# Six half slots for the sparse experts' raw weights, and the dense experts' weights spread between the gathers

## The chip, the cores and the metric

One core of one Trainium2 chip. The metric is the device time of one execution in microseconds (us), as the median of several runs. The engines are TensorE (PE, with its weight loads as PEld), VectorE (DVE), ScalarE (ACT), GpSimd (POOL) and SyncE (SP), which here only issues the weight loads. L584 is line 584 of the kernel before.

## The reference, cut to what matters

Two transformer blocks run one after the other over 256 tokens of 1024 features, in float32. The change touches only the last step of the second block, a mixture of 16 experts in 4 groups:

```python
gsel = jnp.argmax(glog, axis=-1)                       # one group a token
top_p, top_i = lax.top_k(ep, TOPK_IN_GROUP)            # two of its four experts
comb = jnp.sum(jax.nn.one_hot(eid, N_EXPERTS) * wts[..., None], axis=1)
act = jax.nn.silu(jnp.einsum("nd,edf->nef", xt, w1)) * jnp.einsum("nd,edf->nef", xt, w3)
act = act * comb[:, :, None].astype(act.dtype)
y = jnp.einsum("nef,efd->nd", act, w2)                 # D_EXPERT = 256, d = 1024
```

## The kernel before, in words

**Weights.** All weight matrices lie in one stream in HBM, cut into quarters of 128 x 1024 float32. SP loads them two at a time, as halves of 1 MB, into `raw`, a ring of six quarters, so three halves. A quarter is then split in two float32r parts, so that three fast matmul passes give nearly the float32 result: ScalarE rounds it to `w_hi` and another engine subtracts to get `w_lo` (both rings of six quarters as well, with the same index `ring(n)`). In most of the kernel that other engine is GpSimd (L538); in the stage of the sparse experts it is VectorE (`slot_low`, L2381). TensorE's `three` (L962 to 968) issues the three passes; nearly all matmuls have L967. `quarter_done` counts the quarters that TensorE has finished.

**The two dense experts.** Experts 0 and 1 of group 0 are computed for all 256 tokens (`expert_up`, then four row quarters, "the dense down"). Their activations `e_act` are multiplied by each token's weight. For that `comb` is transposed (L1556), stored as `comb_t` (L2361), spread over the partitions with `selectors` (L1561) and multiplied in (L2366); ScalarE rounds to `g_hi` (L918) and VectorE makes `g_lo` (L2372).

**Gathers.** Tokens are sorted by group into 5 tiles of 128 slots: one for each group, and a spare one for a group with more than 128 tokens. One-hot matrices gather the tokens' rows (`tok_hi`, `tok_lo`) into `slot_hi` and `slot_lo`. For each of the 8 feature blocks k a gather of 4 matmuls of 512 columns writes one of banks 4 to 7; ScalarE rounds it (L910), VectorE takes the rest (L2352). After that 8 small gathers of 128 columns do the spare tile (L914, L2357). L1566 gathers the experts' weights for each slot; L2368 sums them to `slot_weight`.

**The sparse experts.** 18 expert slots follow, (tile, expert), each with four up quarters (q0 to q3: gate and up together) and two down quarters. Of these q4 is split like the others; q5, called WHOLE, is used in plain float32 straight from `raw` (L1629, four passes long), so its slot in `raw` is free only when TensorE is done with it. `SLOT_ORDER` puts the down quarters of an expert behind the up quarters of the next: up(0); then up(s), down(s-1) for s = 1 to 17; then down(17). ScalarE and VectorE split four quarters ahead of TensorE (`LEAD`). Between q1 and q2 of up(s) TensorE turns the activations of s-1 (`turn_act`, L1602 to 1607), ScalarE copies them out (L925, L926) and VectorE makes their `g_lo` (L2396). SILU and product are L941 and L2390. At the end matmuls scatter the results back to the tokens (L1639), and a last norm and the store follow.

**Order of the loads.** SP issues in order. Half h of the sparse stage goes to slot (N_HALVES + h) % 3 of `raw` and waits until the half three before it has been used up:

```python
sp.wait_ge(sem("slot_lo_done"), split_count(2 * h - 4))
if SLOT_ORDER[2 * h - 5][1] == WHOLE:
    sp.wait_ge(sem("quarter_done"), N_QUARTERS + 2 * h - 4)
```

Each engine runs its own list in the order in which it is written, so a wait holds back all that stands behind it on that engine.

Of the kernel before, what the change touches and what calls it, by code (L numbers as in the profile page):

```python
# [84 lines left out]
SLOT_HALVES = len(SLOT_ORDER) // 2  # L85

# [5 lines left out]
def split_count(i):  # L92

    return sum(q != WHOLE for _, q in SLOT_ORDER[:i])
# [211 lines left out]
def program(nc, weights, smalls, x_in, p_in, vec_in, rows, con_in, slot_in, sel_in, pos_in, out):  # L306

    ctx = ExitStack()
    with ctx:
# [14 lines left out]
        w_lo = sb("w_lo", RING * QUARTER, F32R)  # L324
        h_hi = sb("h_hi", KD * S, F32R)
# [103 lines left out]
        slot_silu, slot_act = e_act[:, 0:S], e_act[:, S:2 * S]  # L429
        tok_hi = [x[:, 4:8, :].rearrange("p k s -> p (k s)") for x in (g_hi, g_lo)]  # L430
# [58 lines left out]
        def _(sp):  # L489
# [19 lines left out]
            for h in range(SLOT_HALVES):  # L509
                s, q = SLOT_ORDER[2 * h]  # L510
                tile, expert = EXPERT_TILES[s]
                if h < 3:
                    sp.wait_ge(sem("lo_done"), N_QUARTERS + 2 * h - 4)
                else:
                    sp.wait_ge(sem("slot_lo_done"), split_count(2 * h - 4))
                    if SLOT_ORDER[2 * h - 5][1] == WHOLE:
                        sp.wait_ge(sem("quarter_done"), N_QUARTERS + 2 * h - 4)
                at = N_HALVES + 3 * expert + q // 2
                if tile < GROUPS:
                    load_half(at + 3 * GROUP_EXPERTS * tile, (N_HALVES + h) % 3)  # L520
                else:
                    if (expert, q) == (0, 0):
                        sp.wait_ge(sem("overflow_ready"), 1)
                        spare = sp.value_load(overflow_group[0:1, :], min_val=0, max_val=GROUPS - 1)
                    load_half(spare * (3 * GROUP_EXPERTS) + at, (N_HALVES + h) % 3)
# [23 lines left out]
        def _(act_e):  # L549
# [27 lines left out]
            def slot_hi_quarter(i):  # L577
# [4 lines left out]
                act_e.wait_ge(sem(f"half_loaded{n % RING // 2}"), (n // RING + 1) * 16)  # L582
                act_e.wait_ge(sem("quarter_done"), n - (RING - 1))
                nc.scalar.activation(w_hi[:, ring(n)], raw[:, ring(n)], ACT.Copy).then_inc(sem("slot_hi_done"), 1)  # L584
# [323 lines left out]
            for k in range(KD):  # L908
                act_e.wait_ge(sem("gathered"), k + 1)
                nc.scalar.activation(slot_hi[:, k, 0:GROUPS, :], bank[4 + k % 4][:, :].rearrange("p (t c) -> p t c", c=P), ACT.Copy,  # L910
                                     scale=v("norm2", k)).then_inc(sem("slot_h_hi"), 1)
# [4 lines left out]
            for i in range(DENSE):  # L916
                act_e.wait_ge(sem("expert_act_ready"), i + 1)
                nc.scalar.copy(g_hi[:, 2 * i:2 * i + 2, :], e_act[:, i, :]).then_inc(sem("expert_hi_done"), 1)  # L918
# [40 lines left out]
        def _(pe):  # L959
# [579 lines left out]
            expert_up(1)  # L1539
            pe.wait_ge(sem("one_hot_ready"), NT)  # L1540
            pe.wait_ge(sem("tok_lo_done"), NT)
            for k in range(KD):
                if k >= 4:
                    pe.wait_ge(sem("slot_h_lo"), k // 2 * 2 - 2)
                gather(bank[4 + k % 4][:, :], k, slice(0, GROUPS * P)).then_inc(sem("gathered"), 1)
# [7 lines left out]
            pe.wait_ge(sem("pair_free1"), 42)  # L1553
            pe.wait_ge(sem("comb_ready"), NT)
            for t in range(NT):
                ins = nc.tensor.transpose(bank[3][0:N_EXPERTS, t * P:(t + 1) * P], comb[:, t, :], ident)  # L1556
            ins.then_inc(sem("comb_turned"), 1)
            pe.wait_ge(sem("comb_t_stored"), 1)
            pe.wait_ge(sem("selectors_loaded"), 16)
            for e in range(DENSE):  # L1560
                ins = mm(bank[2][:, e * S:(e + 1) * S], selectors[0:N_EXPERTS, e * P:(e + 1) * P], comb_t, start=True, stop=True)  # L1561
            ins.then_inc(sem("comb_spread"), 1)
            pe.wait_ge(sem("comb_slots_ready"), 1)
            for j in range(TILES):
                for t in range(NT):
                    ins = mm(bank[3][:, S + 16 * j:S + 16 * (j + 1)], one_hot[:, t, j * P:(j + 1) * P].bitcast(F32),  # L1566
                             comb_slots[:, t, :], start=t == 0, stop=t == 1)
            ins.then_inc(sem("comb_gathered"), 1)
# [40 lines left out]
            def slot_down(i, s, q):  # L1609
# [14 lines left out]
                else:  # L1624
                    pe.wait_ge(sem(f"half_loaded{n % RING // 2}"), (n // RING + 1) * 16)
                    pe.wait_ge(sem("slot_act_copied"), 2 * s + 2)
                    whole = raw[:, ring(n)]
# [37 lines left out]
        def _(dve):  # L1665
# [684 lines left out]
            for k in range(KD):  # L2350
                dve.wait_ge(sem("slot_h_hi"), k + 1)
                V.scalar_tensor_tensor(slot_lo[:, k, 0:GROUPS, :], bank[4 + k % 4][:, :].rearrange("p (t c) -> p t c", c=P),  # L2352
                                       v("norm2", k), slot_hi[:, k, 0:GROUPS, :].bitcast(F32), ALU.mult, ALU.subtract)\
                    .then_inc(sem("slot_h_lo"), 1)
# [5 lines left out]
            dve.wait_ge(sem("comb_turned"), 1)  # L2360
            V.tensor_copy(comb_t, bank[3][0:N_EXPERTS, 0:S]).then_inc(sem("comb_t_stored"), 1)  # L2361
            dve.wait_ge(sem("comb_spread"), 1)
            for i in range(DENSE):
# [108 lines left out]
```

## Time and profile before

| | us |
|---|---|
| median of 3 runs | 1007.19 |
| lowest, highest | 1005.96, 1010.86 |
| profiled execution | 1007.87 |
| its span in the trace | 1006.1 |
| TensorE busy | 884.3 (88%) |
| VectorE, ScalarE, GpSimd busy | 466.6, 436.5, 470.1 |
| weights moved | 155.20 MB on SP's queue |

A row of a timeline or a group gives the instruction's start and length, what it writes and reads, and in brackets how long its engine sat idle before it and what ended that. The ends of matmuls are modelled: in a stream a 512-column matmul shows 0.39 us, while the next one starts 0.23 us after it. A chain of waits goes back from the last instruction, at each step to what released it. The granted clock is 1.00 at 2.4 GHz and 0.50 at 1.2 GHz. The gathers, the spreading and the dense down stand at 743.6 to 777.2 us, the sparse experts at 777.2 to 990.4 us.

### The profile page before, as it was taken

Reading aid. Unit: us, or ns where it says so; the run is one execution under the profiler, and the core shown is the slowest. Engines: PE = TensorE matmul, PEld = TensorE weight load, DVE = VectorE, ACT = ScalarE, POOL = GpSimd, SP = SyncE. Lnnn points to the kernel's source line nnn. Section 1 sums busy time; section 2 is a strip of 40 time slices with the busy share of each in tenths; the row PEclk is TensorE's granted clock in tenths of the full one; section 3 lists DMA queues with packets and bytes.
Section 4 is the critical chain, followed back from the end, with each engine's and each line's share of the span. In section 5 each row is a group of like instructions: output and inputs, shape, how many; then the busy total and the mean of one; then the engine's idle time right before and its main releaser. Section 6 shows DMA issues by size and latency. Waiting matters only on the chain.

```text
span 1006.1 us, 16140 instructions
## 1 busy us (share of the span) xinstructions
PE 884.3 (88%) x6246; PEld 766.9 (76%) x6246; DVE 466.6 (46%) x962; ACT 436.5 (43%) x676; POOL 470.1 (47%) x372
## 2 busy tenths in 40 slices
PE   4999977999999975999997989989798988888884
PEld 4888867999999864998787989877697765555553
DVE  3723354121112156339456344562784755555643
ACT  5264324454455443534661332333453545445531
POOL 5786664888998954665452233458440000000000
PEclk9999988999999997999988999989897999999998
DMA  7542523555555533243321122235232576766651
GB/s 288 211 146 107 168 100 130 178 200 171 204 168 190 184 126 126 89 164 127 126 85 43 49 80 85 86 126 205 86 127 83 219 305 272 279 262 252 251 209 42
DMA packets 23548, 159.59 MB, mean 159 GB/s; under 512 B 2992, under 2 KB 3520, under 8 KB 4800
## 3 DMA queue, kind: packets, MB, share of 16 engines
q1 hardware_dynamic: 21584, 155.20, 42.3%
q10 hardware_dynamic: 1904, 3.54, 1.0%
q8 instruction: 44, 0.72, 0.3%
q14 instruction: 16, 0.13, 0.0%
HBM read 157.68 MB, written 1.05 MB: 158 GB/s over the span
## 4 chain that ended last, share of the span: by engine, by line
PE 67%; DVE 17%; DMA 9%; ACT 3%; issue 2%; ACTq 0%; SPq 0%; DVEq 0%
PE bank L967 48%; DMA raw<-weights_dram 8%; PE bank L1629 4%; PE bank L1369 3%; DVE w_lo L2381 2%; ACT w_hi L584 2%; PE bank L1056 1%; PE bank L1044 1%; PE bank L1534 1%; DMA row<-dt_bias_dram 1%; DVE work L1755 1%; PE bank L1639 1%; DVE tok L1695 1%; DVE stat L1681 1%; DVE stat L1680 1%
## 5 line engine op out<-in xcount | busy, mean ns | idle before, releaser
L538 POOL TENSOR_TENSOR w_lo<-raw,w_hi 128x512 fp32r<-128x512 f32 x368 | 469.9, 1311 | 274.6 <-ACT w_hi L575 274.3
L967 PE MATMUL bank<-h_hi,w_hi 128*128 128x256 f32 x856 | 250.1, 292 | 0.8 <-POOL w_lo L538 0.8
L967 PE MATMUL bank<-h_lo,w_hi 128*128 128x256 f32 x856 | 243.6, 285 | 0.0
L967 PE MATMUL bank<-h_hi,w_lo 128*128 128x256 f32 x856 | 243.3, 284 | 0.0
L575 ACT ACTIVATE w_hi<-raw 128x1024 fp32r<-128x1024 f32 x184 | 188.6, 1056 | 95.5 <-PE bank L967 80.4
L967 PEld LDWEIGHTS bank<-h_hi,w_hi 128*128 128x128 f32 x856 | 165.4, 193 | 6.3 <-issue 2.5
L967 PEld LDWEIGHTS bank<-h_lo,w_hi 128*128 128x128 f32 x856 | 165.6, 193 | 0.8 <-issue 0.5
L967 PEld LDWEIGHTS bank<-h_hi,w_lo 128*128 128x128 f32 x856 | 165.4, 193 | 0.0
L2381 DVE TENSOR_TENSOR w_lo<-raw,w_hi 128x1024 fp32r<-128x1024 f32 x90 | 106.9, 1221 | 85.3 <-ACT w_hi L584 85.3
L584 ACT ACTIVATE w_hi<-raw 128x1024 fp32r<-128x1024 f32 x90 | 91.7, 1053 | 104.0 <-DMA raw<-weights_dram 92.3
L967 PE MATMUL bank<-w_hi,g_hi 128*128 128x512 f32 x172 | 70.6, 410 | 29.9 <-DVE g_lo L2396 29.0
L1879 DVE SCALAR_TENSOR_TENSOR work<-bank,vec,work 128x255 f32<-128x255 f32 (+1 forms) x44 | 19.2, 478 | 111.1 <-ACT work L664 109.8
L967 PE MATMUL bank<-w_hi,g_lo 128*128 128x512 f32 x172 | 69.6, 405 | 0.0
L967 PE MATMUL bank<-w_lo,g_hi 128*128 128x512 f32 x172 | 69.1, 402 | 0.0
L967 PEld LDWEIGHTS bank<-w_hi,g_hi 128*128 128x128 f32 x172 | 33.3, 194 | 42.8 <-DVE w_lo L2381 28.5
L967 PE MATMUL bank<-w_hi,slot_hi 128*128 128x512 f32 x144 | 65.3, 454 | 0.0
L967 PE MATMUL bank<-w_hi,h_hi 128*128 128x512 f32 (+1 forms) x144 | 56.9, 395 | 4.2 <-issue 2.2
L967 PE MATMUL bank<-w_hi,slot_lo 128*128 128x512 f32 x144 | 56.9, 395 | 0.0
L967 PE MATMUL bank<-w_lo,slot_hi 128*128 128x512 f32 x144 | 56.8, 395 | 0.0
L1044 PE MATMUL bank<-con,tok 128*128 128x128 f32 x80 | 19.0, 418 | 42.7 <-DVE tok L1695 30.7
L967 PE MATMUL bank<-w_lo,h_hi 128*128 128x512 f32 (+1 forms) x144 | 55.1, 383 | 0.0
L967 PE MATMUL bank<-w_hi,h_lo 128*128 128x512 f32 (+1 forms) x144 | 55.1, 383 | 0.0
(347 smaller groups left out, 1311.0 us busy)
## 6 DMA issues: line engine op xcount, KB each, us to landing
raw<-weights_dram SPq DMA_DIRECT2D x146, 1024.0 KB, 4.9
x_sb<-x_dram SPq DMA_DIRECT2D x2, 512.0 KB, 4.7
work<-final_norm_dram ACTq DMA_DIRECT2D x2, 512.0 KB, 4.9
out_dram<-tok SPq DMA_DIRECT2D x1, 1024.0 KB, 4.0
work<-constants_dram ACTq DMA_DIRECT2D x1, 640.0 KB, 6.6
con<-constants_dram ACTq DMA_DIRECT2D x1, 584.0 KB, 5.3
work<-slot_constants_dram ACTq DMA_DIRECT2D x1, 454.0 KB, 5.6
work<-p_dram ACTq DMA_DIRECT2D x1, 256.0 KB, 6.7
```

Of the source, the lines that this page charges most:

```text
L538: ins = nc.gpsimd.tensor_tensor(w_lo[:, part], raw[:, part], w_hi[:, part].bitcast(F32), ALU.subtract)
L575: nc.scalar.activation(w_hi[:, ring(q)], raw[:, ring(q)], ACT.Copy).then_inc(sem("hi_done"), 1)
L584: nc.scalar.activation(w_hi[:, ring(n)], raw[:, ring(n)], ACT.Copy).then_inc(sem("slot_hi_done"), 1)
L967: ins = mm(dst, a, b, start=start and n == 0, stop=stop and n == 2, skip_group_check=True)
L1044: ins = nc.tensor.transpose(bank[4 + k // 2][:, k % 2 * S + t * P:k % 2 * S + (t + 1) * P], tok3[:, t, k * P:(k + 1) * P], ident)
L1056: ins = mm(bank[4 + n % 2][:, t * P:t * P + (t + 1) * P], q3[at:at + HD, f, t * P:(t + 1) * P], k3[at:at + HD, kf(f), 0:(t + 1) * P], star ...
L1369: ins = mm(bank[b][rows, column + m * w:column + (m + 1) * w], lhs[rows, m, :], rhs[rows, m, :], start=True, stop=True)
L1534: ins = mm(dst, x[t][:, k * P:(k + 1) * P], one_hot[:, t, of], start=t == 0 and x is tok_hi, stop=t == 1 and x is tok_lo, skip_group_check ...
L1629: ins = mm(y_banks(tile)[c][:, :], g_whole, whole[:, c * 512:(c + 1) * 512], start=False, stop=last_of_tile(s), skip_group_check=True)
L1639: ins = mm(total[t, c][:, :], one_hot_t[:, tile, t * P:(t + 1) * P], y[:, tile, c * 512:(c + 1) * 512], start=tile == 0 and y is y_hi, sto ...
L1879: ins = V.scalar_tensor_tensor(c, u, fvec("conv_w", (f + j) * 3 + 2 - back), c, ALU.mult, ALU.add)
L2381: V.tensor_tensor(w_lo[:, ring(n)], raw[:, ring(n)], w_hi[:, ring(n)].bitcast(F32), ALU.subtract)\
```

## The change

Two things are changed, both in the mixture of experts. Every computation stays, with its shapes.

First, the raw halves of the sparse stage go round six slots instead of three: the three of `raw`, two in the space of `h_hi` and `h_lo` (here `spare`), free after the dense experts' up projections, and one in `tok`, free after the last gather. Half h waits for what was freed by half h-6, and each slot has its own semaphore. `w_hi` and `w_lo` keep their rings of six quarters.

Second, the transposes of `comb`, the spread, and the gather of the slots' weights move from behind all gathers to between them: the transposes ahead of the first gather, the spread after four, the slots' weights after eight, then the small gathers. VectorE and ScalarE get their parts in a matching order.

```diff
+SLOT_RING = 6
+        def slot_raw(h):
+            r = h % SLOT_RING
+            if r < RING // 2:
+                half = (N_HALVES + r) % (RING // 2)
+                return raw[:, 2 * half * QUARTER:2 * (half + 1) * QUARTER]
+            if r < RING // 2 + 2:
+                return spare[:, (r - RING // 2) * 2 * QUARTER:(r - RING // 2 + 1) * 2 * QUARTER]
+            return tok[:, :]
@@ SP
-                if h < 3:
+                if h < RING // 2:
                     sp.wait_ge(sem("lo_done"), N_QUARTERS + 2 * h - 4)
+                elif h < RING // 2 + 2:
+                    sp.wait_ge(sem("quarter_done"), 4 * (B_MOE + 2))
+                elif h < SLOT_RING:
+                    sp.wait_ge(sem("gathered"), KD + 2)
                 else:
-                    sp.wait_ge(sem("slot_lo_done"), split_count(2 * h - 4))
-                    if SLOT_ORDER[2 * h - 5][1] == WHOLE:
-                        sp.wait_ge(sem("quarter_done"), N_QUARTERS + 2 * h - 4)
+                    freed = 2 * (h - SLOT_RING) + 2
+                    sp.wait_ge(sem("slot_lo_done"), split_count(freed))
+                    if SLOT_ORDER[freed - 1][1] == WHOLE:
+                        sp.wait_ge(sem("quarter_done"), N_QUARTERS + freed)
...
+                sp.dma_start(slot_raw(h), src).then_inc(sem(f"slot_loaded{h % SLOT_RING}"), 16)
@@ ScalarE, slot_hi_quarter
-                act_e.wait_ge(sem(f"half_loaded{n % RING // 2}"), (n // RING + 1) * 16)
+                act_e.wait_ge(sem(f"slot_loaded{i // 2 % SLOT_RING}"), (i // 2 // SLOT_RING + 1) * 16)
                 act_e.wait_ge(sem("quarter_done"), n - (RING - 1))
@@ ScalarE, gathers (rounding of k = 0 to 7; before: all eight, the spare tile, then g_hi)
+            slot_h_first(range(6))
+            for i in range(DENSE):
+                act_e.wait_ge(sem("expert_act_ready"), i + 1)
+                nc.scalar.copy(g_hi[:, 2 * i:2 * i + 2, :], e_act[:, i, :]).then_inc(sem("expert_hi_done"), 1)
+            slot_h_first(range(6, KD))
@@ TensorE (before: all of this behind the small gathers)
+            pe.wait_ge(sem("pair_free1"), 42)
+            pe.wait_ge(sem("comb_ready"), NT)
+            for t in range(NT):
+                ins = nc.tensor.transpose(bank[3][0:N_EXPERTS, t * P:(t + 1) * P], comb[:, t, :], ident)
...
+            gather_groups(range(4))
+            pe.wait_ge(sem("comb_t_stored"), 1)
+            pe.wait_ge(sem("selectors_loaded"), 16)
+            for e in range(DENSE):
+                ins = mm(bank[2][:, e * S:(e + 1) * S], selectors[0:N_EXPERTS, e * P:(e + 1) * P], comb_t, start=True, stop=True)
+            ins.then_inc(sem("comb_spread"), 1)
+            gather_groups(range(4, KD))
+            pe.wait_ge(sem("comb_slots_ready"), 1)
...
+            ins.then_inc(sem("comb_gathered"), 1)
@@ VectorE (before: all slot_lo, then these)
+            dve.wait_ge(sem("comb_turned"), 1)
+            V.tensor_copy(comb_t, bank[3][0:N_EXPERTS, 0:S]).then_inc(sem("comb_t_stored"), 1)
+            slot_h_second(range(4))
+            dve.wait_ge(sem("comb_spread"), 1)
+            (the two products with e_act)
+            slot_h_second(range(4, KD))
+            (g_lo, slot_weight, then the spare tile)
```

## Rows read from the trace of the kernel before

**Rows 1.** The page: granted TensorE clock in 40 equal slices, tenths.

```profile
PEclk9999988999999997999988999989897999999998
```

**Rows 2.** Chain of waits, one expert: start us, us, what.

```profile
813.66 4.79 DMA raw<-weights_dram
818.48 1.07 ACT w_hi L584
819.57 1.22 DVE w_lo L2381
820.80 0.21 DVE g_lo L2396
...
821.15 1.62 PE bank L967 x6
822.77 1.73 PE bank L1629 x4
```

**Rows 3.** Waits, 777 to 990 us: total us, times, longest.

```profile
ACT w_hi L584 <- DMA raw<-weights_dram: 92.3, 49, 5.9
...
PE bank L967 <- DVE g_lo L2396: 29.0, 16, 2.1
```

**Rows 4.** By stretch: us; busy PE, PEld, DVE, ACT, POOL; clock; DMA; GB/s.

```profile
230.00:240.00 10.00, 10.00 (x81) 9.81 (x80) 1.47 (x4) 3.88 (x5) 8.52 (x8) 1.00 0.63 204
743.61:754.57 10.96, 10.96 (x67) 9.46 (x66) 7.73 (x13) 6.65 (x12) 1.33 (x2) 1.00 0.32 114
758.00:764.00 6.00, 5.77 (x24) 4.92 (x22) 1.48 (x4) 3.12 (x4) 0.00 (x0) 0.50 0.00 0
764.75:777.20 12.45, 12.45 (x48) 10.18 (x49) 5.22 (x5) 3.18 (x3) 0.00 (x0) 0.88 0.38 124
782.79:791.85 9.06, 9.06 (x38) 6.75 (x37) 7.01 (x9) 5.92 (x9) 0.00 (x0) 1.00 0.63 233
777.20:990.40 213.20, 184.18 (x691) 129.36 (x689) 118.84 (x134) 102.49 (x153) 0.00 (x0) 0.94 0.63 244
```

**Rows 5.** DMA, 780 to 980 us: 40 slices of 5 us; median landing.

```profile
GB/s 98 321 134 419 138 428 157 387 229 321 311 61 429 165 383 223 184 433 125 433 85 315 315 233 392 36 400 205 334 297 105 424 131 411 190 200 428 100 321 3
...
raw<-weights_dram SPq DMA_DIRECT2D x49, 1024.0 KB, 6.9
```

**Rows 6.** Chain of waits, last scatters and last whole down quarter.

```profile
979.70 5.51 PE bank L1639 x24
...
988.64 1.73 PE bank L1629 x4
```

**Rows 7.** TensorE's timeline after the gathers: start, us, ..., [idle before].

```profile
754.57 0.38 PE L1556 MATMUL bank<-con,work 128*16 128x128 f32 x2
757.43 1.96 PE L1561 MATMUL bank<-work 16*128 16x256 f32 x4 [2.49 <-DVE work L2361]
759.32 4.45 PE L1566 MATMUL bank<-work,one_hot 128*128 128x16 f32 x20
764.75 0.77 PE L967 MATMUL bank<-w_hi,g_hi 128*128 128x512 f32 x1 [0.98 <-issue]
```

**Rows 8.** VectorE's timeline in the gather stage.

```profile
743.64 1.27 DVE L2348 TENSOR_TENSOR work<-work,bank 128x512 f32<-128x512 f32 x2
745.47 0.75 DVE L2352 SCALAR_TENSOR_TENSOR slot_lo<-bank,vec,slot_hi 128x512 fp32r<-128x512 f32 x1 [0.56 <-ACT slot_hi L910]
...
755.94 1.12 DVE L2357 SCALAR_TENSOR_TENSOR slot_lo<-bank,vec,slot_hi 128x128 fp32r<-128x128 f32 x4 [0.66 <-ACT slot_hi L914]
...
763.97 1.28 DVE L2372 TENSOR_TENSOR g_lo<-work,g_hi 128x512 fp32r<-128x512 f32 x2
```

**Rows 9.** ScalarE's timeline in the gather stage.

```profile
744.75 0.69 ACT L910 ACTIVATE slot_hi<-bank,vec 128x512 fp32r<-128x512 f32 x1 [3.18 <-PE bank L1534]
...
754.76 1.14 ACT L914 ACTIVATE slot_hi<-bank,vec 128x128 fp32r<-128x128 f32 x4 [0.65 <-PE bank L1534]
760.15 1.22 ACT L918 CAST g_hi<-work 128x512 fp32r<-128x512 f32 x2 [4.25 <-DVE work L2366]
```

More of the change, by code:

```diff
@@ L1551, in _ @@
                     ins.then_inc(sem("gathered"), 1)
[L1553 to L1568, printed above, removed]
             pe.wait_ge(sem("slot_h_lo"), 2 * KD)
@@ L2349, in _, with slot_h_second @@
                     .then_inc(sem(f"pair_free{1 - i}"), 1)
[L2350 to L2354, printed above, removed]
+            dve.wait_ge(sem("comb_turned"), 1)
+            V.tensor_copy(comb_t, bank[3][0:N_EXPERTS, 0:S]).then_inc(sem("comb_t_stored"), 1)
+            def slot_h_second(ks):
+                for k in ks:
+                    dve.wait_ge(sem("slot_h_hi"), k + 1)
+                    V.scalar_tensor_tensor(slot_lo[:, k, 0:GROUPS, :], bank[4 + k % 4][:, :].rearrange("p (t c) -> p t c", c=P),
+                                           v("norm2", k), slot_hi[:, k, 0:GROUPS, :].bitcast(F32), ALU.mult, ALU.subtract)\
+                        .then_inc(sem("slot_h_lo"), 1)
+            slot_h_second(range(4))
+            dve.wait_ge(sem("comb_spread"), 1)
+            for i in range(DENSE):
+                dve.wait_ge(sem(f"pair_free{1 - i}"), 42 + 2 * i)
+                x = e_act[:, i, :].rearrange("p (f s) -> p f s", s=S)
+                V.tensor_tensor(x, x, each_of(bank[2][:, i * S:(i + 1) * S], 2), ALU.mult).then_inc(sem("expert_act_ready"), 1)
+            slot_h_second(range(4, KD))
+            for i in range(DENSE):
+                dve.wait_ge(sem("expert_hi_done"), i + 1)
+                V.tensor_tensor(g_lo[:, 2 * i:2 * i + 2, :], e_act[:, i, :].rearrange("p (f s) -> p f s", s=S),
+                                g_hi[:, 2 * i:2 * i + 2, :].bitcast(F32), ALU.subtract).then_inc(sem("expert_lo_done"), 1)
+            dve.wait_ge(sem("comb_gathered"), 1)
+            V.tensor_reduce(slot_weight, bank[3][:, S:S + 16 * TILES].rearrange("p (t g e) -> p t e g", t=TILES, g=GROUPS),
+                            AX_X, ALU.add).then_inc(sem("slot_weights_ready"), 1)
             for k in range(KD):
@@ L2359, in _ @@
                     .then_inc(sem("slot_h_lo"), 1)
[L2360 to L2363, printed above, removed]
-                dve.wait_ge(sem(f"pair_free{1 - i}"), 42 + 2 * i)
-                x = e_act[:, i, :].rearrange("p (f s) -> p f s", s=S)
-                V.tensor_tensor(x, x, each_of(bank[2][:, i * S:(i + 1) * S], 2), ALU.mult).then_inc(sem("expert_act_ready"), 1)
-            dve.wait_ge(sem("comb_gathered"), 1)
-            V.tensor_reduce(slot_weight, bank[3][:, S:S + 16 * TILES].rearrange("p (t g e) -> p t e g", t=TILES, g=GROUPS),
-                            AX_X, ALU.add).then_inc(sem("slot_weights_ready"), 1)
-            for i in range(DENSE):
-                dve.wait_ge(sem("expert_hi_done"), i + 1)
-                V.tensor_tensor(g_lo[:, 2 * i:2 * i + 2, :], e_act[:, i, :].rearrange("p (f s) -> p f s", s=S),
-                                g_hi[:, 2 * i:2 * i + 2, :].bitcast(F32), ALU.subtract).then_inc(sem("expert_lo_done"), 1)
             def slot_low(i):
```

45 lines of the change are left out of this document (27 added, 18 removed).

## The prediction

> **What bounds the kernel now.** I read the page's clock line first [rows 1], then the chain of waits, then who waited for whom, then busy time by stretch. The page's slices 31 to 39 (755 to 980 us) are the stage of the sparse experts (18 expert slots of three weight halves, 1 MB each). There the granted clock often reads 8 or 9 tenths, where it reads 9 (full) for most of the middle of the kernel.
>
> The chain through one expert [rows 2] is a loop: the whole-float32 quarter of a down projection ends at 813.60, only then does the next half start to load (4.79 us), then ScalarE rounds it (1.07), VectorE takes the rest (1.22), a small g_lo product follows (0.21), TensorE does the down quarter (1.62) and the whole quarter (1.73) to 824.50. That is 10.9 us a turn, and 4.8 of it is a load with nothing in front of it: the half that is wanted next has no free slot until the last one has been used up. The waits say the same [rows 3]: ScalarE waits 92.3 us for loads in 49 waits, and TensorE's idle of 29.0 us is put down to g_lo, the last link of that loop, in 16 waits of up to 2.1 us.
>
> The stretches give the price [rows 4]. From 777.20 to 990.40 TensorE is busy 184.2 of 213.2 us at a mean clock of 0.94. So 29 us are idle, and 0.06 x 213 = 13 us are what running part of the stage at 1.2 instead of 2.4 GHz costs. One turn without idle and at full clock is in the trace: 782.79 to 791.85, 9.06 us, TensorE busy 9.06, VectorE 7.01, ScalarE 5.92. Where TensorE is fed without gaps the clock reads 1.00 (230 to 240 us, and both stretches of full busy time in the gathers and that turn). The Trainium skill says (TensorE: Matmul & The Clock Gate, "What's actually happening") that the lower clock is the array's default and activity releases it; by that rule the 13 us come back with the idle, and the trace agrees in these stretches.
>
> **Part 1, six half slots.** Nothing is removed or added on TensorE, ScalarE or VectorE; 54 loads of the same size stay. What moves is when a load may be issued: half h waits for what freed half h-6, not h-3. Six halves are two experts. In the order of the stage the TensorE's turn is up(s) q0 to q3, down(s-1), whole(s-1). A down half of s-1 waits now for whole(s-3). Call that time T. Behind it in SP's queue stand the two up halves of s+1, whose slots were freed a little before T, so three halves are asked for at about T. Median time to landing with halves in the queue is 6.9 us, and slices of 5 us in this stage moved 428 to 433 GB/s [rows 5], so the three (3.15 MB) need 7.35 us plus the start. Alone, one lands after 4.8 us [rows 2]. The down half is read by ScalarE and VectorE (2.3 us) before TensorE reaches it, at T + 9.06 + 5.8 = T + 14.9. It lands at about T + 5, so 7 to 8 us of cover are left. The up halves of s+1 are wanted at T + 18.1 and land by about T + 10; 6 us of cover. So the load leaves the chain. What is late next? Per turn DMA needs 7.35 us, VectorE 7.01, ScalarE 5.92, TensorE 9.06. TensorE is. The ring of six split quarters is unchanged and runs four quarters ahead; in-order ScalarE does its silu after q3, with the next quarter to be split needed 5.9 us of TensorE work later against about 3.2 us of work (silu 0.4, rounding 1.07, product 0.5, low part 1.22; the first and third are estimates for 256 columns, between ScalarE's 0.28 for 128 and 0.69 for 512 in the rows of part 2), so that should hide too.
>
> The stage then takes: up of the first slot 782.79 - 777.20 = 5.6; 17 turns x 9.06 = 154.0; the end, scatters to the last whole quarter, 979.70 to 990.37 [rows 6], 10.7; five turns that also turn a one-hot tile, two transposes more (0.38 for two at most, [rows 7]; in a stream half of that, the ends being modelled), about 0.2 each, 1.1. Sum 171.4 against 213.2: **41.8 us gained**. Bounds: with the clock not coming back, 13 less; with an added hand-over of 0.3 us a turn, 5 less; it can't be more than about 1 us better, since 9.06 has no idle in it.
>
> A rule that speaks against this: the Trainium skill (SBUF — State Buffer, "Summary: rules for kernel authors") says to reckon with some 358 GB/s for HBM to SBUF. By it three halves take 8.79 us, 0.27 under TensorE's turn, and the sum is the same but with almost no cover. The measured 428 GB/s over whole 5 us slices of this very stage speaks for the higher rate.
>
> The loads issued early cost nothing. Halves 3 and 4 go to the space of h, free when the second dense up ends (743.6); half 5 goes to tok and waits for the last gather, and half 6 on are queued behind it on SP. They wait for nothing lost: half 6 needs the low part of the second slot quarter, which is made beside the dense down. The DMA engines were idle there (0.00 share at 758 to 764, [rows 4]).
>
> **Part 2, the spreading between the gathers.** Before: the gathers run 743.61 to 754.57, then two transposes, 2.49 idle for VectorE's copy of comb_t (queued behind all its slot_lo work), the spread 1.96, the slot weights 4.45 to 763.77, 0.98 idle, and the dense down at 764.75 [rows 7]. The last four items ran at half clock: 0.50 at 758 to 764 [rows 4].
>
> After: TensorE waits first for pair_free1 at 42, the first of the two dense products, which ends 743.64 + 0.64 = 744.3 [rows 8], where before it began at 743.6; everything is queued behind it, price 0.7. The transposes add 0.4: 744.7. Then the same gathers, 10.96, the spread and the slot weights in between. These now stand inside busy time, so at full clock half of 1.96 and of 4.45: 0.98 and 2.2 (bounds: these, or the full 6.4). Sum 744.7 + 10.96 + 3.2 = 758.8. The new waits between gathers: comb_t is copied while four gathers run (3.7). Gather k=6 needs slot_lo of k=3, at about 748.4 + 0.7 + 0.75 + handing over = 750.1 [rows 8, 9], and TensorE comes there at about 751.2. On ScalarE the two g_hi roundings (1.22) stand before k=6 and 7, on VectorE the two products (1.28) before slot_lo of k=4; both have ended before the last gather (VectorE 11.4 us of work, ScalarE 9, in 16.6), so no wait of TensorE comes of them, by estimate. After the last gather the tail stays: 754.57 to the last slot_lo at 755.94 + 1.12 = 757.06, 2.5 us. Then the dense down can begin at 761.3 instead of 764.75, as g_lo and its two roundings have long been done: **3.4 us gained**; bounds 0.2 (everything in between at half clock) and 4.1 (the first wait free).
>
> The dense down took 12.45 at mean clock 0.88 [rows 4], because it began at half clock. Idle of 2.5 us stands just before it in the new order too, as before the drop in the old one, so I leave it at 12.45. Bounds 10.95 (12.45 x 0.88) and 14.
>
> **The sum.** The profiled execution took 1007.87, its span 1006.1. 1007.87 - 41.8 - 3.4 = 962.7. The median of the runs shown is 1007.19, 0.7 less, so **962** for the median after.
>
> **Rivals.**
> A, forecast (TensorE bounds every turn): 962, own range 957 to 968 by the bounds of part 2, the dense down and a few tenths of hand-over in a turn. Chance 0.77.
> B, the loads bound: each turn waits for 3.15 MB at a sustained rate below 3.15/9.06 = 347 GB/s. For it: no long stretch of the stage moved more, and slices such as 315, 315 in a row occur. Against: those fall where nothing was asked for, and full slices reach 428 [rows 5]. At 315 a turn is 9.99, 17 x 0.93 = 16 more: 978. It would show as ScalarE still waiting for slot loads. Chance 0.10.
> C, the clock doesn't come back: the stage has no idle yet keeps stretches at 1.2 GHz: 13 more, 975. Against it 1.00 at 230 to 240 with TensorE full. Chance 0.05.
> D, it doesn't do what it says: SP issues in order, the down half's wait holds back the up halves behind it, and the loads land as late as before. Only part 2 is left: 1003.8. Against: 7 us of cover worked out above. Chance 0.04, with a half-way 985 in it.
> E, slower: with three loads always in the queue, into three separate areas, the sustained rate falls so far that a turn is longer than now. The point: the stage may take 213.2 + 3.4 = 216.6, less the 17.4 outside the turns, over 17 turns, 11.7 us, that is 269 GB/s. At 250 GB/s a turn is 12.6, 17 x 0.9 = 15 us over that point: 1022. For it: landing rises from 4.8 to 6.9 us as loads overlap; against: that is sharing, and the rate rises with it [rows 5]. Chance 0.03. The last 0.01 is for nothing changed.
>
> **How the numbers follow.** A measurement of this kernel can tell about 0.5%, 5 us, from no change. A, B, C, most of D are faster by more: 0.96. D's full case lies 3.4 us below: same 0.02. E: slower 0.02. Range: A with C, and the milder half of B, low 957, high 976; left out are the rest of B, D and E, some 0.12, and what A's range may miss.
>
> **What would show it.** In the trace after: ScalarE's wait for slot loads falls from 92 us to under 10; TensorE has no 2 us waits for g_lo; a turn of 9.1 to 9.3 us; granted clock 1.00 from about 775 on; DMA at a steady 310 to 350 GB/s rather than 430 and 100 in turns. The dense down begins at about 761. The end from the last whole quarter (990.37 before) to the end of the span stays 15.7 us. Wrong if turns stay above 9.6, if SP's queue still asks for each half just before ScalarE wants it, or if waits of 1 us and more stand between the gathers.

## The result, and the profile after

| us | before | after |
|---|---|---|
| median of 4 runs each, side by side | 1007.77 | 972.96 |
| lowest, highest | 1005.96, 1010.86 | 971.08, 974.85 |
| profiled execution | 1007.87 | 974.85 |

The ratio is 0.965, interval 0.961 to 0.969. The forecast was 962, range 957 to 976. A later comparison of the same two programs gave 963.69 (962.14 to 971.99, 5 runs) against 1008.49 and a ratio of 0.954 (0.948 to 0.961). The experiments show where the two medians differ.

Part 1 is to be seen in the chain of waits of after, one expert (start us, us, what), that answers to [rows 2]:

```profile
848.92 2.80 PE bank L995 x12
851.72 0.11 PE bank L1635
851.83 0.11 PE bank L1640
851.93 4.16 PE bank L995 x18
856.10 1.72 PE bank L1662 x4
```

From 848.92 to 857.81, where the next one starts, it is 8.89 us, and every piece is TensorE's: two up quarters, the turning of the activation, two up quarters and the down quarter (18 matmuls), the whole quarter. Load, rounding and g_lo have left the chain. The first five turns, which also turn a one-hot tile, take 9.10 to 9.14 and the eleven behind them 8.88 to 8.91.

The waits of after from 740 to 960 us (us in total, times, longest), to be held beside [rows 3]:

```profile
ACT g_hi L953 <- PE bank L1640: 49.6, 18, 8.4
...
ACT w_hi L607 <- PE bank L995: 10.5, 6, 4.9
...
PE bank L995 <- DVE slot_lo L2410: 2.4, 1, 2.4
...
PE bank L1578 <- DVE work L2381: 1.3, 1, 1.3
```

ScalarE's 92.3 us of waiting for loads are gone. What it waits for now is TensorE: the turned activation (49.6 us) and a free quarter of the ring (10.5). TensorE's 16 waits for g_lo are gone too. Ahead of the last whole quarter it waits twice, both times in the gather stage: 1.3 us before the transposes and 2.4 us before the dense down.

By stretch (columns as in [rows 4]): gathers and spreading, dense down to the last whole quarter, the first 5 us of the dense down, and the turn above.

```profile
753.97:775.23 21.26, 17.64 (x90) 15.35 (x91) 12.87 (x26) 9.83 (x20) 1.77 (x2) 0.80 0.48 182
775.23:957.35 182.12, 182.10 (x738) 136.28 (x738) 124.75 (x138) 105.41 (x156) 0.00 (x0) 0.99 0.72 281
775.00:780.00 5.00, 4.77 (x11) 3.81 (x12) 2.44 (x3) 0.91 (x1) 0.00 (x0) 0.50 0.69 254
848.92:857.81 8.89, 8.89 (x37) 6.57 (x37) 7.99 (x10) 7.42 (x11) 0.00 (x0) 1.00 0.87 341
```

The second row is the main result. TensorE is busy for 182.10 of 182.12 us. The same two events stood 225.6 us apart before (764.75 to 990.37, [rows 6, 7]): 43.5 us less. The first row is the disappointment: from the start of the gather stage to the dense down it is 21.26 us, where it was 21.15 (743.6 to 764.75). The third shows the dense down begin at half clock.

The chain through that stage, which answers to [rows 7]:

```profile
754.47 0.69 DVE work L2381
...
755.20 0.39 PE bank L1578 x2
755.59 3.72 PE bank L1562 x16
759.31 1.05 PE bank L1586 x4
760.36 3.92 PE bank L1562 x16
764.28 2.14 PE bank L1592 x20
766.42 6.43 PE bank L1562 x32
...
773.14 0.89 ACT slot_hi L945 x3
...
774.05 1.14 DVE slot_lo L2410 x4
```

The spread (L1586) takes 1.05 and the slots' weights (L1592) 2.14, both at full clock as forecast. But the 32 small gathers behind them take 6.43 us; before, they were the last part of 10.97 us of gathers, about 3.5 (an estimate: 32 starts 0.11 us apart, the step that the rows below show ahead of 766.9). TensorE's timeline shows the place and the step of the clock. There is no idle of TensorE ahead of it since the transposes began at 755.20:

```profile
764.12 2.30 PE L1592 MATMUL bank<-work,one_hot 128*128 128x16 f32 x20
...
766.75 0.32 PE L1562 MATMUL bank<-one_hot,g_hi 128*128 128x128 f32 x1
766.87 0.42 PE L1562 MATMUL bank<-one_hot,tok_lo 128*128 128x128 f32 x1
767.09 0.41 PE L1562 MATMUL bank<-one_hot,g_lo 128*128 128x128 f32 x1
```

From 766.9 on a 128-column matmul of the gathers starts every 0.21 us instead of every 0.11.

The clock line of the page, and the DMA line from 760 to 960 us (40 slices of 5 us) with the median times to landing, answer to [rows 1, 5]:

```profile
PEclk9999988999999999799998898988989799999998
```

```profile
GB/s 408 7 29 254 136 210 16 378 51 398 274 431 285 419 277 388 326 331 364 306 360 364 433 288 403 329 328 387 310 426 287 419 288 377 364 62 3 0 0 0
...
raw<-weights_dram SPq DMA_DIRECT2D x24, 1024.0 KB, 7.0
spare<-weights_dram SPq DMA_DIRECT2D x16, 1024.0 KB, 5.3
tok<-weights_dram SPq DMA_DIRECT2D x9, 1024.0 KB, 6.9
```

The clock line can't show what the sparse experts gained: in slices 32 to 39 (780 to 981 us) it read 9 before as well, since a 9 is anything from 90% up, and the mean there was 0.94. In after it has a 7 in slice 32 (754 to 778 us, the fall above) and 9 in the seven slices behind it; the window rows say 0.99. It also has more 8s ahead of that, eight instead of six, in code that the change doesn't touch. The tail is as it was (957.35 to the span's end at 973.1, 15.7 us).

So the profiled times differ like this. The gather stage begins 10.4 us later (753.97 against 743.6), its length differs by 0.1, and from the dense down on 43.5 us are gained: 33.0 in all, 1007.87 to 974.85.

### The profile page after: what moved, and what is told of

Same layout as the page of the kernel before. It is cut to its first block, busy times and chain, and to the rows that moved or that the text cites. A ratio compares the mean times of both kernels' runs of the same rounds, so it can differ in the third digit from the quotient of the medians.

```text
span 973.1 us, 16139 instructions
## 1 busy us (share of the span) xinstructions
PE 880.5 (90%) x6246; PEld 773.4 (79%) x6246; DVE 471.8 (48%) x962; ACT 435.8 (45%) x676; POOL 467.0 (48%) x372
## 3 DMA queue, kind: packets, MB, share of 16 engines
HBM read 157.68 MB, written 1.05 MB: 163 GB/s over the span
## 4 chain that ended last, share of the span: by engine, by line
PE 79%; DVE 13%; issue 4%; POOL 3%; ACT 1%; DVEq 0%; POOLq 0%; ACTq 0%
PE bank L995 59%; PE bank L1662 3%; POOL w_lo L561 3%; PE bank L1397 3%; PE bank L1562 1%; PE bank L1072 1%; PE bank L1084 1%; PE bank L1672 1%; DVE stat L1714 1%; DVE stat L1713 1%; DVE work L1948 1%; PE bank L1095 1%; DVE stat L1715 1%; DVE bank L2087 1%; PE bank L1103 1%
## 5 line engine op out<-in xcount | busy, mean ns | idle before, releaser
L598 ACT ACTIVATE w_hi<-raw 128x1024 fp32r<-128x1024 f32 x184 | 188.7, 1056 | 98.1 <-PE bank L995 83.3
L995 PEld LDWEIGHTS bank<-h_hi,w_hi 128*128 128x128 f32 x856 | 167.8, 196 | 7.4 <-issue 3.1
L995 PEld LDWEIGHTS bank<-h_lo,w_hi 128*128 128x128 f32 x856 | 168.2, 196 | 0.8 <-issue 0.5
L995 PEld LDWEIGHTS bank<-h_hi,w_lo 128*128 128x128 f32 x856 | 167.9, 196 | 0.0
L1912 DVE SCALAR_TENSOR_TENSOR work<-bank,vec,work 128x255 f32<-128x255 f32 (+1 forms) x44 | 19.2, 478 | 111.3 <-ACT work L687 109.9
L2420 DVE TENSOR_TENSOR w_lo<-raw,w_hi 128x1024 fp32r<-128x1024 f32 x46 | 54.0, 1220 | 13.4 <-ACT w_hi L607 13.4
L1072 PE MATMUL bank<-con,tok 128*128 128x128 f32 x80 | 19.5, 424 | 43.5 <-DVE tok L1728 30.7
L1072 PEld LDWEIGHTS bank<-con,tok 128*128 128x128 f32 x80 | 16.2, 222 | 46.4 <-issue 25.2
L607 ACT ACTIVATE w_hi<-raw 128x1024 fp32r<-128x1024 f32 x46 | 46.0, 1058 | 9.9 <-PE bank L995 9.9
```

The source lines that it names most:

```text
L598: nc.scalar.activation(w_hi[:, ring(q)], raw[:, ring(q)], ACT.Copy).then_inc(sem("hi_done"), 1)
L607: nc.scalar.activation(w_hi[:, ring(n)], slot_quarter(i), ACT.Copy).then_inc(sem("slot_hi_done"), 1)
L995: ins = mm(dst, a, b, start=start and n == 0, stop=stop and n == 2, skip_group_check=True)
L1072: ins = nc.tensor.transpose(bank[4 + k // 2][:, k % 2 * S + t * P:k % 2 * S + (t + 1) * P], tok3[:, t, k * P:(k + 1) * P], ident)
L1912: ins = V.scalar_tensor_tensor(c, u, fvec("conv_w", (f + j) * 3 + 2 - back), c, ALU.mult, ALU.add)
L2420: V.tensor_tensor(w_lo[:, ring(n)], slot_quarter(i), w_hi[:, ring(n)].bitcast(F32), ALU.subtract)\
```

## The experiments

### Each part alone, the same program again, and one step moved

Four kernels ran beside a before of 1008.49 (1004.44 to 1017.37, 13 runs). **slots_only** is the six slots with the old order of gathers and spreading; **spread_only** is the new order with three slots; **after_again** is the changed kernel once more. In **weights_last** the slots' weights stand behind all gathers:

```
             gather_groups(range(4, KD))
-            [wait for comb_slots_ready, 20 matmuls of the slots' weights]
             for k in range(KD):
                 ...
                 ins = gather(bank[4 + k // 4][...], k, slice(GROUPS * P, SLOTS))
+            [wait for comb_slots_ready, 20 matmuls of the slots' weights]
```

and VectorE's sum of them (slot_weight) behind its last slot_lo.

> Only the six slots; the spreading stays behind the gathers. Theory T1 (the six slots carry the whole gain; the moved spreading is worth nothing because the clock falls to 1.2 GHz in it): from the start of the dense down to the last whole quarter about 182 us as in the changed kernel (225.6 before), the gathers and the spreading 21.2 us as before, time within 3 us of the changed kernel, 970 to 975 us. Rival T2 (the moved spreading is worth the 3.4 us of the forecast, and something else ate it): 3 to 4 us slower than the changed kernel, about 976 us.

> Only the spreading between the gathers, with three slots. T1: within 1 us or so of the kernel before, about 1007 us, and 21 us from the end of the dense up projections to the start of the dense down. T2: 3.4 us faster, about 1004 us.

> The changed kernel once more, unedited, for where TensorE's clock is low in the part ahead of the mixture of experts, which the change doesn't touch but which ended 10.4 us later in its profile. Theory P (chance: the low stretches fall differently in each execution of the same program): another set of low stretches than in the first profile, and the end of the dense up projections anywhere from 743 to 755 us. Rival Q (it comes with the program built): the same set, dense up ending at 753 to 755 us again.

> The changed kernel with the gather of the slots' weights (20 small float32 passes) moved behind the small gathers. Theory R (these small passes let the clock fall at 766.7 us; behind them the small gathers took 6.4 instead of 3.5 us): small gathers at full clock, 3.5 us, and the weights' gather stands in the 2.4 us in which TensorE waited for the last slot_lo; the dense down begins 4 to 5 us earlier, about 968 us. Rival S (the clock would fall at that point whatever runs, since it fell by its own rhythm): the small gathers stay at 6 us or the fall comes just behind, and only the 2 us of cover are gained, about 971 us.

**Measured.** slots_only 964.79 (963.22 to 973.47, 4 runs), ratio 0.959 (0.951 to 0.967). spread_only 1010.92 (1004.37 to 1017.19, 10 runs), ratio 1.000 (0.995 to 1.005). after_again 963.69 (5 runs). weights_last 958.92 (957.86, 958.82, 959.02, 968.23), ratio 0.954 (0.946 to 0.962).

**What follows.** Nearly the whole gain is the slots'. slots_only has the cleanest reading, since its profiled run begins the gather stage at 743.80, as before's did:

```profile
743.80:764.92 21.12, 17.65 (x92) 14.94 (x91) 12.63 (x25) 10.92 (x20) 1.86 (x2) 0.83 0.57 218
764.92:945.70 180.78, 180.78 (x738) 135.37 (x738) 125.19 (x139) 104.71 (x155) 0.00 (x0) 0.99 0.71 279
```

Dense down to last whole quarter is 180.8 instead of 225.6: 44.8 us. The medians alone could not show the forecast 3.4 us of the spreading, since the interval of spread_only's ratio is 5 us wide to each side. Its profile shows that they aren't there: from the last up quarter to the dense down it is 20.5 us (751.5 to 772.02) against 21.15. It has the same fall behind the slots' weights, which end at 763.75 (a window of spread_only):

```profile
765.00:770.00 5.00, 4.63 (x22) 4.44 (x21) 1.13 (x4) 1.47 (x6) 0.00 (x0) 0.50 0.00 0
```

All six profiles with this order have the fall, 0.4 to 2.0 us behind the end of the slots' weights: after, after_again, spread_only, five_slots, four_slots_b and third_more. Where it comes latest, in four_slots_b and third_more, the small gathers take 5.0 us instead of 6.4, and the stretch from the last up quarter to the dense down takes 19.2 us (a line of four_slots_b's chain):

```profile
757.38 4.98 PE bank L1562 x32
```

So the moved spreading is worth 0 to 2 us of the forecast 3.4, as the fall happens to lie. With the same work in the other order, the windows of weights_last from the first gather to the dense down, and behind it, read:

```profile
746.11:760.73 14.62, 14.42 (x89) 12.22 (x88) 11.01 (x23) 9.83 (x20) 0.17 (x1) 1.00 0.63 239
760.73:773.10 12.37, 12.37 (x54) 10.25 (x55) 5.96 (x7) 4.92 (x5) 0.00 (x0) 1.00 0.61 228
```

From the transposes (745.73, ahead of the window) to the dense down it is 15.0 us instead of 20.0 in after (755.20 to 775.23), and the clock stays at 1.00 to the end of the stage. Most runs of the two kernels, 962.1 to 964.8 and 957.9 to 959.0, stand about 5 us apart. The fall isn't there either in filled, below, which has this order too and a first wait as long as after's (1.24 us). So that this fall comes of the place of the 16-column matmuls is shown; how the chip decides on it is not.

### Why one program has two times

after_again and the run of after are the same program, yet the runs stand in two groups: 962.1 to 964.8 and 971 to 975. The before's 13 runs spread over 1004.4 to 1017.4. **before_again** profiled the kernel before once more.

> The kernel before once more, for its low stretches ahead of the mixture of experts. Theory P (they differ between executions of the same program, and decide most of the scatter): a time above 1010 comes with a sum of low stretches there above the 58 us of the first profile, a time near 1005 with about 58 or less. Rival Q: the same stretches whatever the time.

**Measured.** One run, 1016.85. It begins its gather stage at 753.17, where the first profile did at 743.6. Two windows of that untouched code, of the first profile:

```profile
590.00:600.00 10.00, 9.18 (x182) 8.57 (x182) 5.79 (x17) 1.88 (x3) 4.98 (x4) 1.00 0.31 107
645.00:655.00 10.00, 10.00 (x97) 9.93 (x93) 8.31 (x14) 4.25 (x7) 5.66 (x5) 1.00 0.15 61
```

and of before_again:

```profile
590.00:600.00 10.00, 7.70 (x78) 7.26 (x78) 4.68 (x12) 2.50 (x6) 2.78 (x4) 0.66 0.00 0
645.00:655.00 10.00, 8.66 (x88) 8.23 (x88) 4.20 (x11) 0.67 (x1) 4.79 (x4) 0.66 0.61 210
```

**What follows.** In some executions the clock falls at places where in others it doesn't. Added up from windows of 5 us, the time at 1.2 GHz ahead of 745 us is 58 us in the profiles of before and slots_only, 65 in four_slots_b and weights_last, and 78 to 82 in before_again, after, after_again and five_slots. The 20 us more of before_again are worth at most 10 (an estimate: half of them), and it begins the stage 9.6 us later; 1.4 of these are there by 31 us, ahead of any fall, because a small load landed after 11.33 us instead of 10.02.

Compare profiles with alike sums: 1007.87 with 963.22 (slots_only) is 44.7, and 1016.85 with 971.99 (after_again) is 44.9. Of the second difference 2.2 us lie ahead of the gather stage (the last up quarter ends at 751.1 instead of 753.3), so the change itself is worth 42.6 there, and 43.4 between after and before. The forecast was 45.2. That the first two profiles stand only 33.0 us apart, and 10.4 of the 12.2 us between the forecast for the profiled run (962.7) and its 974.85, come of the later start and not of the change. What makes one execution fall where another doesn't stays open.

### How much room the loads have, and how many slots it takes

**five_slots** (beside a before of 1010.27) and **four_slots_b** (beside 1010.91) have one and two slots fewer. **third_more** (beside 1010.27) has five slots, and with every third half SP loads one more MB, which nobody reads, into the space of the sixth:

```
-SLOT_RING = 6
+SLOT_RING = 5
...
+                if h >= 6 and h % 3 == 0:
+                    [wait for the last gather, and for the extra load before]
+                    sp.dma_start(tok[:, :], more).then_inc(sem("more"), 16)
```

> Five slots instead of six, and every third half is followed by one more load of 1 MB, into tok, that nobody needs: 4.19 MB a turn instead of 3.15. It measures what the loads can do when TensorE doesn't hold them back. If the sustained rate is the 428 GB/s of the best 5 us slices, a turn becomes 9.8 us, and the 16 turns that have one cost some 12 us more: about 975. If it is 385 GB/s: 10.9 us a turn, 30 us more, about 992. By the Trainium skill (SBUF - State Buffer, Summary: rules for kernel authors), some 358 GB/s for HBM to SBUF, it would be 11.7 us a turn, 43 us more, about 1005.

> Only SLOT_RING = 5 (tok isn't used). Theory: with about 7 us of cover at six slots, one slot less (half a turn of about 3 us less lead) still hides every load: same time as the changed kernel, 962 to 972 us, turns of 8.9 to 9.1 us. Rival (the six slots are just enough): turns of 9.3 us and more, 5 us or more slower.

> SLOT_RING = 4 (the three of raw and one in the space of h): half h waits for what half h-4 freed, one and a third turns. Theory (what counts is the lead against landing plus splitting): a load is asked for at least a third of a turn earlier than with three slots, so most of the 4.8 us is hidden but not the queue of two or three loads (7 us); turns of 9.1 to 9.8 us, 965 to 985 us. Rival (any slot above three is enough, because it takes off the one wait on the whole quarter that mattered): as with five and six, low clock alike, 963 to 973.

**Measured.** third_more 977.65 (976.62 to 988.54), ratio 0.969 (0.961 to 0.978). five_slots 972.78 (963.87, 972.38, 973.19, 974.78), ratio 0.959 (0.951 to 0.967). four_slots_b 969.38 (964.42, 964.62, 974.13, 974.65), ratio 0.963 (0.954 to 0.972).

DMA line of third_more, 780 to 940 us (40 slices of 4 us), and one turn's piece of its chain, the extra load, which the next follows at 850.45:

```profile
GB/s 139 403 100 254 422 424 426 422 416 426 416 424 424 422 422 422 426 414 418 422 424 420 424 420 424 412 424 424 418 420 422 424 422 422 416 420 422 420 424 426
```

```profile
840.50 9.86 DMA tok<-weights_dram
```

**What follows.** With a load always queued, three areas and four halves a turn, the queue holds about 422 GB/s from 796 us to the end of the line, 144 us. A turn is then 9.93 us, 4.19 MB at 422 GB/s. Three halves need 7.45 us at that rate, of a turn of 8.89. So rival B had 1.4 us of room. The Trainium skill (SBUF — State Buffer, "Summary: rules for kernel authors") says to reckon with some 358 GB/s for HBM to SBUF, by which four halves would take 11.7 us (an estimate from its figure). The chain shows 9.9, with one core at work, and the measurement decides.

The number of slots above three hardly matters. From the end of the first whole quarter to the last scatters' start, the sixteen turns take 143.4 us with six slots, 143.4 with five and 143.6 with four. (Three of the five slots' runs, 972.4 to 974.8, stand in the later group; the profiled one of them begins the stage within 0.5 us of after_again's, and ends 0.4 us later.) four_slots_b waits for loads again (its waits from 775 to 950 us), but its chain repeats every 8.9 us (activation turned at 849.95 and 858.86), the six slots' turn:

```profile
ACT w_hi L607 <- DMA raw<-weights_dram: 24.0, 31, 2.9
...
ACT w_hi L607 <- DMA spare<-weights_dram: 8.7, 11, 2.4
```

32.7 us of waiting, nearly all hidden behind TensorE, in the same engine that waited 92.3 us before when it was on the chain. The medians of these few runs don't tell four, five and six slots apart. What one slot more removes is the bond of a load to the end of the turn.

### Idle time filled with dummy matmuls

Three kernels put matmuls whose result nobody reads in front of TensorE's waits. **filled** is weights_last with 118 of them in four waits upstream (ahead of three norms and one gating step). **gathers_first** is filled with the transposes behind the second gather and the spread behind the sixth. **before_filled** is the kernel before with seven (1.6 us) in most turns, ahead of the down quarter:

```
                 if q == 4:
+                    if expert >= 1 and s < len(EXPERT_TILES) - 1:
+                        ...
+                        for _ in range(7):
+                            mm(bank[4 + 2 * ((tile + 1) % 2)][:, :], g_hi[:, 4, 0:P], g_hi[:, 4:6, :], start=True, stop=True, ...)
                     pe.wait_ge(sem("slot_lo_done"), split_count(i + 1))
```

> On the version with the weights' gather last: dummy matmuls, whose results nobody reads, in four waits of TensorE ahead of the mixture of experts: 24 ahead of mix_turn(4), 22 ahead of norm_turn(1), 50 ahead of norm_turn(3), 22 ahead of norm_turn(4). They add no work to other engines. Theory (idle lets the clock fall, and what follows pays for it): the low stretches that follow these four waits go (two of 6.8 us, one of 10.2, one of 6.8 in the profile of weights_last's kind), up to 15 us of low clock come back at half, time 948 to 953 us against 958.9. Rival (the clock falls anyway, or the filling is itself in the way): 957 to 962 us.

> On filled (weights' gather last, four waits filled): the transposes of comb move from ahead of the first gather to behind the second, the spread to behind the sixth. Theory (the first wait costs what the forecast called 0.7 and the profile showed as 1.2 us): 1 to 1.5 us faster than filled, about 954.5 us. Rival (the wait only moves, since VectorE's row of slot_lo is then what the gathers wait for): same as filled, 955.8.

> The kernel before, with three slots, and 7 dummy matmuls of 512 columns (1.6 us) ahead of the down quarter in 13 of its 17 turns, where TensorE waits 1.6 to 2.1 us for the loop of load, rounding and low part. The loads are as late as before. It tells the two parts of the gain apart. Theory (29 us were idle and 13 us were low clock that the idle brings): in the stage the six falls of 3.4 us go or become fewer, and 8 to 10 us come back, 998 to 1002 us, while the loop itself stays at 10.9 us a turn. Rival (the clock falls by its own rhythm): no gain, 1008 us or more.

**Measured.** filled 955.78 (954.13 to 961.12), ratio 0.945 (0.938 to 0.952): the lowest median, with an interval that overlaps that of weights_last. gathers_first 958.49 (956.75 to 961.05), ratio 0.951 (0.945 to 0.958). before_filled 1009.21 (1005.03 to 1016.80, 10 runs) beside 1010.91 (13 runs), ratio 1.002 (0.997 to 1.006).

**filled.** The time at 1.2 GHz ahead of 745 us fell from 65 us (weights_last) to 37.5, yet little of it came back. At the start of the router's small operations filled is 3.4 us ahead (717.47 against 720.82). Lines of VectorE's timeline, of filled:

```profile
720.43 0.16 DVE L2329 TENSOR_REDUCE work<-work 128x2 f32<-128x8 f32 x1
...
722.84 1.34 DVE L2336 TENSOR_SCALAR work<-work 128x8 f32<-128x8 f32 x1
724.22 2.45 DVE L2339 TENSOR_TENSOR work<-work 128x16 f32<-128x16 f32 x2
```

and of weights_last:

```profile
725.23 0.16 DVE L2328 TENSOR_SCALAR work<-work 128x8 f32<-128x8 f32 x1
725.42 1.24 DVE L2331 TENSOR_TENSOR work<-work 128x16 f32<-128x16 f32 x2
```

In filled GpSimd makes eight w_lo splits in a row here (717.81 to 727.86, 1.3 us each). VectorE's tiny elementwise operations beside them take 1.0 to 1.3 us, and each ends within 0.03 us of the end of a split; after 730 us, alone, the same kind takes 0.16 to 0.19. The reductions beside the splits still take 0.16. In weights_last the splits begin 2.4 us later, and three operations slip in where one split follows another (0.29, 0.16 and 0.16 us). Both kernels end this piece at 726.7, and filled's lead is gone. It gets 1.1 back in the next (tok_lo of the second tile 1.21 instead of 2.30). So the clock was worth little there, since VectorE's chain sets the end.

**gathers_first** does hide the first wait: from the last up quarter to the dense down it is 14.8 us (743.3 to 758.10) against 16.2 in filled (742.5 to 758.75). But the clock falls around the start of its dense down, as these windows of it show and none of filled does:

```profile
755.00:760.00 5.00, 4.80 (x32) 4.31 (x32) 4.21 (x11) 3.13 (x7) 0.00 (x0) 0.79 0.61 210
760.00:765.00 5.00, 5.00 (x21) 4.04 (x20) 1.66 (x2) 1.06 (x1) 0.00 (x0) 0.87 0.58 210
```

The 1.4 us are gone by the end of the stage (181.2 us from dense down to last whole quarter against 179.7).

**before_filled.** The falls in the sparse stage are fewer, against the rival of a clock with its own rhythm, but the time isn't lower, against the theory. These windows of before, and of before_filled, hold one fall each; before has seven between 830 and 980 us, before_filled only this one, which is longer:

```profile
855.00:860.00 5.00, 3.88 (x8) 2.47 (x9) 3.93 (x6) 3.87 (x5) 0.00 (x0) 0.66 0.53 223
```

```profile
865.00:870.00 5.00, 2.05 (x5) 1.49 (x5) 2.36 (x3) 3.40 (x6) 0.00 (x0) 0.75 0.72 301
870.00:875.00 5.00, 5.00 (x11) 2.61 (x10) 4.09 (x5) 2.26 (x3) 0.00 (x0) 0.57 0.00 0
```

In before, two turns with one fall last 23.5 to 24.0 us and two without 21.8, some 2 us a fall. (before_again, with one fall fewer than before, is 2.0 us shorter over its sixteen turns: 185.9 against 187.9.) But the sixteen turns of before_filled take 184.1, 3.8 less than before's, where one long fall instead of seven should give some 10 (an estimate: five falls' worth of low clock at 2 us each). Its chain shows where the rest went:

```profile
825.06 6.56 DMA raw<-weights_dram
...
834.31 1.62 PE bank L967 x6
835.94 1.72 PE bank L1637 x4
```

The load in the chain takes 5.4 to 6.6 us in five turns, where it took 4.7 to 5.0 in fourteen of before's sixteen; that up halves asked for at another time now share the queue is argued, not shown. Ahead of the turns 2.8 us are lost (1.6 of it the first seven dummies, 1.2 a dense down with a longer fall). From dense down to the last whole quarter it is 224.6 against 225.6. So with three slots this filling returns about nothing: what fewer falls give back goes again in longer loads and in the dummies themselves. The split is read from one profile of each; the medians (ratio 1.002) show only the sum.

## Why the prediction came out as it did

**Part 1, the direction and mechanism: right.** By its own list, ScalarE's wait for slot loads fell to 0 (forecast under 10), the g_lo waits are gone, the clock is 1.00 from 785 us on, the tail is 15.7 as before. DMA is not at a steady 310 to 350 GB/s in slices of 5 us: from 805 to 935 us it still swings from 274 to 433, since three halves at 422 GB/s (third_more) need 7.45 of the 8.89 us of a turn. The mean in the turn above is 341. One reading was wrong and carried nothing: the page's slices 31 to 39 don't "often" read 8 or 9; slice 31 reads 7 and slices 32 to 39 all read 9. The 0.94 comes from the window row.

**Part 1, the size: 41.8 forecast, 44.8 alone (slots_only), 43.5 in the profile of after.** The step that was off is 17 x 9.06, with the floor that it was called ("it can't be more than about 1 us better"). The turn was read from the start of its first matmul (782.79) to the end of its last (791.85), and the ends are modelled late. From end to end it is 8.89, since the matmul ahead of it ends at 782.96 (TensorE's timeline of before):

```profile
782.57 0.39 PE L967 MATMUL bank<-w_hi,slot_lo 128*128 128x512 f32 x1
782.79 0.39 PE L967 MATMUL bank<-w_hi,slot_hi 128*128 128x512 f32 x1
```

Sixteen turns were summed at 9.06 plus 1.1 for one-hots, 146.1; they took 143.4 in after: 45.6 for the five with a one-hot, 97.8 for the eleven without. The turn is 8.89 here too, and the one-hots add the forecast 0.2. The profile of after gives 1.0 back in the dense down, which began at half clock (26.4 us from its start to the first whole quarter, before and slots_only 25.4 and 25.3). "I leave it at 12.45" was right only where the fall comes as early as before.

**Part 2: 3.4 forecast, nothing measured in after** (21.26 against 21.15), and 0 to 2 in the other profiles of this order. The parts, from the chain of after: the first wait took 1.25 (TensorE's last up quarter ends at 753.95, transposes at 755.20) instead of 0.7, because VectorE began its first product 0.5 us late. The spread took 1.05 and the weights 2.14, as forecast 0.98 and 2.2. The tail is 2.4 (forecast 2.5). Then comes the step that failed: "the same gathers, 10.96". They were taken at full clock because they stand inside busy time. Their last 32 took 6.43 instead of about 3.5, 2.9 us, and this is the whole of the missing 3.4 with the longer first wait. The lower bound, 0.2, "everything in between at half clock", looked for the half clock in the moved matmuls; it fell on those behind them. The Trainium skill (TensorE: Matmul & The Clock Gate, "What's actually happening") says that the lower clock is the array's default and activity releases it, and I read "busy" for activity. TensorE was busy without a gap from 755.20 to 766.9, and the clock fell all the same, so a busy share of 1.0 in a window, as in [rows 4], doesn't prove that the clock stays. In weights_last it is 15.6 us from the last up quarter to the dense down (745.1 to 760.73) against 21.15 before, since the slots' weights now also lie beside the last slot_lo work, in what was TensorE's wait of 2.4.

**The median: 973 or 964 against 962.** The forecast took the first profile (58 us at 1.2 GHz ahead of the stage) for the program. The three runs shown, 1005.96 to 1010.86, gave no sign that one program can stand 10 us apart; the later runs of before, 1001 to 1018, do. The range reached 976 by rival C's price, not because of this cause, so that 972.96 lies in it is luck. The change itself was forecast at 45.2 and is worth 43.4 in the profile of after: part 1 gave 1.7 more, part 2 3.5 less, and that the sum is so near is partly luck too.

**The rivals.** B (loads bound): excluded with a number: 422 GB/s sustained where 347 were needed. C (clock doesn't come back): it came back, 0.99 from the dense down on. What of its 13 us is the clock's alone isn't known: in before_filled, with three slots, fewer falls brought no lower time. D (it doesn't do what it says): excluded by the waits. E: the rate did not fall with three areas in the queue, it rose to its steady 422.

## What to carry to other kernels

When the chain of one turn holds a load that starts only as the last step of the turn ends, one more slot takes the load off the chain, and further slots bought almost nothing here; measure the next engine's turn from the same edge to the same edge, end to end or start to start, since 0.17 us of a modelled end counts 17 times. Very short matmuls put into the middle of a stream can slow down what stands behind them: try them where the stream ends anyway, and look at the clock in windows behind the moved work, not only at its own time. Before reading a difference of 1% between two profiles, compare the start time of the first stage that the change touches, and take it off.

## What was new about the hardware

- The clock fell to 1.2 GHz with no idle of TensorE ahead of the fall, behind twenty 16-column matmuls (764.12 to 766.4, fall at 766.8 in after; the same, 0.4 to 2.0 us behind them, in the five other profiles of this order). With these twenty at the end of the gathers it stayed at 1.00 in weights_last and filled; gathers_first had one fall of 3.4 us at the start of the dense down.
- One program on one core has executions 10 us apart (962 and 972; 1005 and 1017), for the most part by more or longer falls of the clock in the same code (58 us at 1.2 GHz ahead of 745 us in one profile of before, 78 in the other).
- One core's loads of 1 MB held 422 GB/s for 144 us (third_more), with TensorE, VectorE and ScalarE at work.
- VectorE's elementwise operations on 8 to 16 columns took 0.16 to 0.19 us alone and 1.0 to 1.3 us beside GpSimd operations of 1.3 us, ending with them, while reductions beside them took 0.16 (filled).
